# A hybrid decoder trunk on one Trainium2 core: x brought token-major by VectorE blocks and a DRAM round trip in place of TensorE transposes

## The reference

```python
z = zxbcdt[..., :D_INNER]
xbc = zxbcdt[..., D_INNER:D_INNER + CONV_DIM]
xbc = silu(causal_dwconv(xbc, conv_w, conv_b))
xs = xbc[..., :D_INNER].reshape(b, s, N_GROUPS, HEADS_PER_GROUP, HEAD_DIM)
bm, cm = ...
xdt = x * dtc[..., None]
y_diag = einsum("bcgls,bcgrls,bcsgrp->bclgrp", cb, decay, xdt)
states = einsum("bclgn,bcgrl,bclgrp->bcgrpn", bc, decay_to_end, xdt)
...
y = y_diag + y_off + d_skip * xs
```

## Time and profile before

| | |
|---|---|
| three runs, median (lowest to highest) | 1107.18 us (1107.04 to 1107.32) |
| the profiled execution | 1107.1 us |
| its span, first to last instruction | 1105.3 us |
| mean granted TensorE clock | 0.998 |
| PE busy | 1093.8 us, 99% of the span |
| DVE, ACT, POOL busy | 570.3, 468.5, 593.3 us |
| DMA queue of SP | 115.83 MB, 31.3% of 16 engines |

### The profile page before, as it was taken

The page is one execution under the profiler, slowest core; times in us unless marked ns, Lnnn a source line. Parts: engine busy times, 40 slices in busy tenths (PEclk is TensorE's granted clock), DMA queues, the critical chain, the costliest instruction groups (busy, mean ns, idle before and its releaser), DMA issues.

```text
span 1105.3 us, 15325 instructions
## 1 busy us (share of the span) xinstructions
PE 1093.8 (99%) x5156; PEld 898.0 (81%) x5156; DVE 570.3 (52%) x640; ACT 468.5 (42%) x804; POOL 593.3 (54%) x448
## 2 busy tenths in 40 slices
PE   9999999999999999999999999999999999999997
PEld 7788888888888788788788878888888888888886
DVE  5665421455423284666777856666664224554123
ACT  7433222233333338558595774343332222333332
POOL 3766544444565635337364474656665444445653
PEclk9999999999999999999999999999999999999999
DMA  7223232222222225333324333222222222323232
GB/s 286 83 99 103 89 101 96 95 95 95 95 95 95 95 77 156 126 105 124 130 92 141 122 107 106 96 95 95 95 95 95 95 95 95 98 99 101 93 104 77
DMA packets 40085, 117.05 MB, mean 106 GB/s; under 512 B 4080, under 2 KB 11888, under 8 KB 40048
## 3 DMA queue, kind: packets, MB, share of 16 engines
q1 hardware_dynamic: 39616, 115.83, 31.3%
q10 hardware_dynamic: 432, 0.73, 0.2%
HBM read 114.32 MB, written 2.23 MB: 105 GB/s over the span
## 4 chain that ended last, share of the span: by engine, by line
PE 97%; DMA 1%; DVE 1%; POOL 1%; issue 0%; ACT 0%; ACTq 0%; DVEq 0%; POOLq 0%
PE bank L832 30%; PE bank L833 30%; PE bank L834 30%; PE bank L1023 1%; PE bank L1032 1%; PE bank L1040 1%; DMA params<-params 1%; PE bank L982 1%; PE bank L873 1%; POOL residual L739 0%; PE bank L1000 0%; PE bank L853 0%; PE bank L961 0%; PE bank L991 0%; DVE residual L1223 0%
## 5 line engine op out<-in xcount | busy, mean ns | idle before, releaser
L712 POOL TENSOR_TENSOR w_lo<-w_raw,w_hi 128x512 fp32r<-128x512 f32 x372 | 499.4, 1348 | 464.2 <-ACT w_hi L437 451.8
L437 ACT ACTIVATE w_hi<-w_raw 128x512 fp32r<-128x512 f32 x372 | 230.6, 626 | 403.9 <-PE bank L834 397.7
L832 PE MATMUL bank<-x_hi,w_hi 128*128 128x512 f32 x848 | 336.1, 396 | 1.7 <-DVE x_lo L1133 1.5
L834 PE MATMUL bank<-x_hi,w_lo 128*128 128x512 f32 x848 | 330.6, 390 | 0.0
L833 PE MATMUL bank<-x_lo,w_hi 128*128 128x512 f32 x848 | 330.5, 390 | 0.0
L832 PE MATMUL bank<-act_hi,w_hi 128*128 128x512 f32 (+1 forms) x656 | 254.5, 388 | 0.0
L834 PE MATMUL bank<-act_hi,w_lo 128*128 128x512 f32 (+1 forms) x656 | 252.2, 384 | 0.0
L833 PE MATMUL bank<-act_lo,w_hi 128*128 128x512 f32 (+1 forms) x656 | 252.1, 384 | 0.0
L832 PEld LDWEIGHTS bank<-x_hi,w_hi 128*128 128x128 f32 x848 | 159.3, 188 | 39.2 <-issue 4.9
L833 PEld LDWEIGHTS bank<-x_lo,w_hi 128*128 128x128 f32 x848 | 159.4, 188 | 34.1 <-issue 2.1
L834 PEld LDWEIGHTS bank<-x_hi,w_lo 128*128 128x128 f32 x848 | 159.3, 188 | 33.3
(11 more groups left out here) (154 smaller groups left out, 683.4 us busy)
## 6 DMA issues: line engine op xcount, KB each, us to landing
w_raw<-weights SPq DMA_DIRECT2D x186, 512.0 KB, 3.3
m<-acs_scratch SPq DMA_DIRECT2D x16, 512.0 KB, 4.4
decay_in<-eacs_scratch SPq DMA_DIRECT2D x24, 128.0 KB, 3.7
x_token<-x_tok SPq DMA_DIRECT2D x4, 512.0 KB, 6.3
residual<-xt SPq DMA_DIRECT2D x8, 256.0 KB, 9.9
out_first<-scaled_residual SPq DMA_DIRECT2D x4, 256.0 KB, 2.4
out_second<-output_rows SPq DMA_DIRECT2D x4, 256.0 KB, 2.7
pooling_matrices<-pooling ACTq DMA_DIRECT2D x2, 288.0 KB, 5.1
```

Of the source, the lines that this page charges most:

```text
L437: act.activation(whi[:, c % 2, part], raw[:, c % 2, part], ACT.Copy).then_inc(hi_ready, 1)
L712: pool.tensor_tensor(wlo[:, c % 2, part], raw[:, c % 2, part], whi_f[:, c % 2, part], ALU.subtract).then_inc(lo_ready, 1)
L832: pe.matmul(out, wh, xh, start=start, stop=False)
L834: return pe.matmul(out, wl, xh, start=False, stop=stop)
```

## The change

The six convolved units of a group come in the order x0, x1, x2, x3, B, C. So x of group g + 1 is ready at t = 8 of group g. There ACT applies silu to x (before the weights of its ninth unit), and DVE transposes it in blocks of 32x32 (`transpose_blocks`, four instructions) between the scaling and the taps of B's convolution. The blocks go to the group's free tiles of `y_accumulated`. At t = 8 SP writes them to a DRAM scratch in four DMAs of 32 partitions (rows of 512 B), and at t = 9 it reads all 1 MB back with one DMA (rows of 2 KB), token-major, into the same tiles. x_dt is made from there, in two instructions a chunk, and the fourth chunk's stands behind the product m*cb of chunk 0. The skip, which overwrites these tiles, moves from t = 0 to t = 3. The product m*cb of chunk 3 moves ahead of the after-chunk work at t = 8. PE's transposes of x go, with their waits; waits of the chunks on earlier chunks are set anew. For group 0 the same is done in the fifth of the six first units, and the read stands on SP behind the writes of the decay scratch and one weight load.

```diff
-T_TOKEN, T_LATE_TOKEN = 1, 2
+T_TOKEN = 1
+Q = 32
...
+        x_dram = nc.dram_tensor("x_scratch", [GROUPS, CHUNKS * (P // Q), Q, P // Q, GT * Q], F32).ap()
...
+        def x_blocks(g):
+            return yx[:, GT * g:GT * g + GT, :].rearrange("p i t -> p (i t)").rearrange("p (n f) -> p n f", f=GT * Q)
...
+            def write_blocks(g):
+                sp.wait_ge(xt_blocks, g + 1)
+                blocks = x_blocks(g)
+                for a in range(P // Q):
+                    sp.dma_start(x_dram[g, :, :, a, :].rearrange("n q f -> q n f"),
+                                 blocks[Q * a:Q * a + Q, :, :]).then_inc(xt_written, 16)
+            def read_tokens(g):
+                sp.wait_ge(xt_written, 16 * (P // Q) * (g + 1))
+                sp.dma_start(yx[:, GT * g:GT * g + GT, :],
+                             x_dram[g].rearrange("(c b) q a f -> (b q) c (a f)", c=CHUNKS)
+                             ).then_inc(xt_landed, 16)
...
             for u in range(5):
                 load_ahead(u)
+            write_blocks(0)
             sp.wait_ge(acsf_ready, 1)
...
             load_ahead(5)
+            read_tokens(0)
             sp.wait_ge(scratch, 2 * GROUPS * 16)
...
+                    if t == 8 and g + 1 < GROUPS:
+                        write_blocks(g + 1)
+                    if t == 9 and g + 1 < GROUPS:
+                        read_tokens(g + 1)
...
+                if u == 4:
+                    silu_x(0)
                 first_tap(u)
...
             def skip(g):
-                act.wait_ge(x_act, g + 1)
+                act.wait_ge(xdt_ready, 4 * g + 4)
...
                     u = slot_of(g, t)
+                    if not ends and t == 8:
+                        silu_x(g + 1)
                     ahead(u, 0)
                     if t == 0:
                         silu_b_c(g)
-                        silu_x(g)
...
-                    if t == 0:
+                    if t == 3:
                         skip(g)
...
-                pe.wait_ge(x_act, g + 1)
-                if g == 0:
...
-                for c in range(CHUNKS - 1):
-                    token_x(g, c)
...
-                    if t == T_LATE_TOKEN:
-                        pe.wait_ge(bt_ready, g + 1)
-                        token_x(g, CHUNKS - 1)
...
+            def transpose_blocks(g):
+                dve.wait_ge(x_act, g + 1)
+                blocks = x_blocks(g)
+                for i in range(GT):
+                    last = dve.transpose(blocks[:, :, Q * i:Q * i + Q],
+                                         xact[:, i, :].rearrange("p (n j) -> p n j", j=Q))
+                last.then_inc(xt_blocks, 1)
...
                 conv_scale(u)
+                if u == 4:
+                    transpose_blocks(0)
                 conv_taps(u)
...
-                dve.wait_ge(x_mm, 4 * g + c + 1)
-                dve.tensor_tensor(by_head(xdt[:, c, :]), by_head(XT_BANK[c][:, :]),
+                dve.wait_ge(xt_landed, 16 * (g + 1))
...
+                for half in range(2):
+                    last = dve.tensor_tensor(out[:, half], landed[:, half],
+                                             dt[:, half].unsqueeze(2).unsqueeze(3).to_broadcast([P, GT, 2, Q]),
+                                             ALU.mult)
+                last.then_inc(xdt_ready, 1)
...
                         token_x(g, 2)
-                    if t == 3:
-                        token_x(g, 3)
...
+                    if t == 8:
+                        decay_times_cb(g, TIMES_CB_IN[t])
...
-                    if t in TIMES_CB_IN:
+                    if t in TIMES_CB_IN and t != 8:
...
                         conv_scale(CONVS * (g + 1) + t - GT)
+                        if t == 8:
+                            transpose_blocks(g + 1)
...
                         decay_times_cb(g, 0)
+                        token_x(g, 3)
...
-        return np.r_[b0 - x0 + g * P:b0 - x0 + (g + 1) * P, c0 - x0 + g * P:c0 - x0 + (g + 1) * P,
-                     g * gw:(g + 1) * gw]
+        return np.r_[g * gw:(g + 1) * gw, b0 - x0 + g * P:b0 - x0 + (g + 1) * P,
+                     c0 - x0 + g * P:c0 - x0 + (g + 1) * P]
```

46 lines of the change are left out of this document (23 added, 23 removed).

## The result

The changed kernel takes 1111.09 us (median of 14 runs, 1108.86 to 1112.08) against 1107.32 us (14 runs, 1107.04 to 1107.47): a ratio of 1.0031, 95% interval 1.0023 to 1.0039. It is slower; 1101.0 was predicted. The profiled execution took 1111.8 us with a span of 1110.0, 4.7 us over the span before.

The account below looks back on a forecast made before the run. PE, busy 1093.8 of 1105.3 us, was taken as the bound. 1107.1 less 6.76 saved, plus 0.6 wait in group 3, is 1100.9; the median stands 0.08 above, so 1101.0. Forecast ends 1100.3 to 1104.3; stated range 1100.3 to 1106.0.

Parts of the forecast that it names:

- PE's saving, 6.76 us: On PE, 64 transposes of x removed: 1.69 us a group, 6.76 for four.
- Block transposes at 0.62: On DVE, four 32x32-block transposes of 128x512 a group at 0.62 us each, 2.48 a group added.
- the rival of dear transposes: On DVE, block transposes as dear as RECIPROCAL, 3.35 us each: 1140.7 us, slower; chance 0.09.
- x_dt starts at 569.82, needs 2.2 and a z product of 0.7, and is done by 572.7: On DVE in group 2, ahead of the first product m*cb: x_dt's six halves stay hidden behind ACT's exponentials.
- The half's price, 0.36: On DVE, one x_dt half from SBUF: half of 0.62 plus a little, 0.36 us; six halves 2.2.
- a cover of 1.9: On DVE ahead of the first product: six x_dt halves could take 1.9 us more and stay hidden.
- the gain is given back: Rival on DVE: transposes at 1.24 us, or x_dt halves waiting for GpSimd; 1106.5, no change; chance 0.13 (1104.3 to 1109).
- DVE enters 1.64 later: On DVE from t = 8: transposes of 2.48 us less the 0.84 gap they fill; group 2's gate ends at 568.70.
- DVE follows PE through the middle of the group: In group 2, this moves group 3's product end from 643.99 to 642.30, before other delays.
- The skip at t = 3: On ACT, moved from t = 0; holds group 2's first y addition, adding 0 to 2.55 us, taken as 0.9.
- The start: Group 0: m lands 431.1 to 434.4, product ends 437.5 to 440.8, PE comes at 440.33; no wait, 0.5 at the end.
- Late x: Rival: x's way through DRAM adds 8 us, PE waits 0.4, 2.5, 3.5 in groups 1 to 3: 1106.8; chance 0.09.

Follow-up runs that it names:

- x5: The kernel before, with one PE transpose of x a chunk instead of four (16 instead of 64): 1102.50 us, ratio 0.9956.
- x1: The changed kernel with only chunk 0's x_dt ahead of the product, and GpSimd's decayed copy of chunk 1 behind t = 2's weight residues: 1108.46 us, ratio 1.0014.
- x13: The changed kernel with x_dt made with one SBUF input, eight instructions of 64 columns a chunk instead of two of 256: 1124.59 us, ratio 1.0158.
- x4: The changed kernel with x_dt in one instruction of 512 columns a chunk instead of two, tiles strided by four elements: 1117.15 us, ratio 1.0088.

## Why the prediction was wrong

- **PE's saving, 6.76 us: right.** x5 gives 4.76 for the 4.8 that its part comes to, and group 1's first y_diag product stands at 507.06 without a wait.
- **Block transposes at 0.62: right.** Four take 2.48 us, mean 0.678, no more than a copy of that size; the rival of dear transposes is out. Here the trace agrees with what the Trainium skill's "Vector Engine (DVE) Microarchitecture Reference", 3.8, states of them.
- **The step that failed: "x_dt starts at 569.82, needs 2.2 and a z product of 0.7, and is done by 572.7, so it stays hidden behind the exponentials."** The half's price, 0.36 worked out from a PSUM-source row, is near it alone (0.41) and far off beside GpSimd (1.26 to 1.51): the six took 5.98 us, 3.8 more, against a cover of 1.9. The rival "the gain is given back" named this very mechanism; I gave it 0.13, since six halves have 1.9 us of cover, and let it end at 1109. The row it rested on, L1332 at 1.54 to 2.31, had the price in it: alone it takes 1.21 us (at 549.64 before), so one that meets GpSimd costs up to 1.1 us more, and six halves up to 6.6.
- **"DVE enters 1.64 later": too little, the second step that failed.** The gate ended 11.09 us ahead of PE before (567.06 to 578.15) and 6.05 now (567.57 to 573.62): 5.04 nearer, 1.69 of it PE's own saving in the group, so DVE was 3.35 late by this count and 3.31 by its own starts (x5 above). That DVE follows PE through the middle of the group held: it was 2.80 us early at t = 7 of group 1. The transposes cost 1.43, near the 1.64 priced. What I had at nothing is the rest, 1.9 us: the state scaling, a y addition and the gate meet GpSimd and are dearer beside it too.
- **The skip at t = 3**, priced at 0.9 between 0 and 2.55: it cost nothing. DVE waited 1.42 us for it in group 1 and 0.30 in group 2, and then stood idle for PE, 1.53 and 3.52 us, ahead of the scaling of t = 4.
- **The clock** had no term. It cost 4.3 us behind the two waits of the profiled execution: by this ledger the change would have come out with no difference without it. The three runs with a mean of 0.997 were still some 1.5 us slower than before, and no profile of one was taken.
- **The start: right.** ACT took m at 434.36, in the 431.1 to 434.4 worked out, and PE waited 0.17 us.
- **Late x: out.** In groups 1 to 3 x_dt never waited for the DMA; in group 0 it did for 3.0 us, hidden there. In group 2 the first of the four writes was issued at 552.12 and the read, which waits for all four, at 558.56, 6.4 us later, 3.18 of them the four issues. The 5.5 us that I estimated from the Trainium skill's "SBUF — State Buffer", Door 1, are neither borne out nor refuted by that.

What stays open: whether the change's x_dt could be had at its price alone in groups 1 to 3, since a kernel in which GpSimd is idle in that stretch wasn't tried; and how the loss divides in the runs that weren't profiled.

## What to carry to other kernels

When an edit moves an operand from PSUM to SBUF, price the instruction beside what GpSimd does at that place, not alone: here 0.41 us became 1.26 to 1.51. Work that leaves the engine on the path shortens the run only if the engines that feed it can follow. Here DVE followed until it came to lie beside other instructions of GpSimd, and had no idle time to take these delays up: read busy time by stretches of a group, not of the span. And a wait on PE can cost more in its clock: 1.6 to 2.7 us behind waits of 3.33 us here, nothing behind 2.00 in x1, so a change near break-even on waits can come out slower.

## What the runs showed of the hardware

- A DVE instruction with two SBUF inputs that starts beside a GpSimd TENSOR_TENSOR ends a fixed time behind it: 0.28 us with 256 columns (alone 0.41), 0.55 with 512 (alone 0.68; 544.72 + 1.79 against 543.83 + 2.13), 1.08 with 1024 (alone 1.21; before, 532.87 + 2.31 against 534.10). The pieces of 64 columns in x13 end 0.05 behind it (alone 0.24). It looks as if DVE waits GpSimd's instruction out and then does its columns; so splitting makes the work dearer, by one wait for each GpSimd instruction that it meets.
- It goes both ways: a GpSimd TENSOR_TENSOR that starts beside such a DVE instruction is late as well (the residue at 543.83, beside the product at 543.58, took 2.13 us, 1.30 elsewhere).
- A DVE instruction with one input from PSUM (0.68) and the block transpose (0.68) keep their price beside GpSimd.
- An element stride of 16 bytes took 1.09 instead of 0.68 us both as a block transpose's output (x4) and as PE's moving operand.
- With waits of 3.33 us PE's granted clock fell to 0.50 (1.2 GHz), from 576 to 582 us in group 2 and from 651 to 654 us in group 3; with 2.00 and 1.98 us in the profiled execution of x1 it stayed at 1.00. I had not reckoned with it at all.
